# adaLN vectors from w_ada as the moving operand, in column chunks, with q, k, v of the first four attention passes run role by role

## What is computed

```python
ada = silu(c) @ w_ada + b_ada                    # c: 1024 values of this sequence; w_ada: 1024 x 3072
shift, scale, gate = split(ada, 3)
h = rms_norm(x, norm_g) * (1 + scale) + shift
z = h @ w_in                                     # 1024 -> 8704 columns
# branch A: three groups of 8 heads x 64, (window, dilation) = (128,1), (512,4), (2048,16)
q, k = partial_rope(rms_norm(q)), partial_rope(rms_norm(k))
o, lse = dilated_window_attention(q, k, v)       # the groups are combined by their softmax denominators
y_a = attn * silu(z_gateA)
# branch B: chunked spatial gating, y_b = u * (W_s v + b) * silu(z_gateB)
merged = sigmoid(z_mA) * (y_a @ w_branch_a) + sigmoid(z_mB) * (y_b @ w_branch_b)
out = x + gate * (merged @ w_out)
```

## Time and profile before

| what | us |
|---|---|
| median of 6 runs | 961.58 (960.37 to 964.3) |
| the profiled execution, its own time | 961.78 |
| span of its slowest core, first to last instruction | 960.2 |
| PE busy in that span | 812.4 |
| DVE, ACT, POOL busy | 489.4, 409.0, 309.0 |

### The profile page before, as it was taken

How to read it: one execution, slowest core, us unless ns; L and a number is a source line. 1 busy time by engine, 2 the same in 40 slices (tenths; PEclk the granted TensorE clock), 3 DMA queues, 4 the chain that set the end, 5 groups by cost and what they waited for, 6 DMA issues and landing times.

```text
span 960.2 us, 15418 instructions; the slowest of 8 cores (952.5 to 960.2 us)
## 1 busy us (share of the span) xinstructions
PE 812.4 (85%) x5088; PEld 419.4 (44%) x5088; DVE 489.4 (51%) x811; ACT 409.0 (43%) x695; POOL 309.0 (32%) x356
## 2 busy tenths in 40 slices
PE   0895568667899999999999965698876999999997
PEld 0895223233455555544444431243432444444443
DVE  5102346566677777766677654446652432222343
ACT  2103244445466666656666653276663212121100
POOL 0000342344233442332212200624342433332576
PEclk9999887889899999999999987698988999999999
DMA  8980101100082900020000000890005922231396
GB/s 186 335 159 0 44 23 45 45 23 1 1 119 41 151 13 2 1 40 6 2 1 2 1 1 1 91 151 1 1 0 134 218 23 23 23 34 11 117 303 238
DMA packets 53823, 62.63 MB, mean 65 GB/s; under 512 B 31472, under 2 KB 43888, under 8 KB 52720
## 3 DMA queue, kind: packets, MB, share of 16 engines
q0 software_dynamic: 42944, 22.47, 19.3%
q1 hardware_dynamic: 8496, 30.78, 10.4%
q10 hardware_dynamic: 2304, 8.39, 2.1%
HBM read 75.70 MB, written 8.39 MB: 88 GB/s over the span
## 4 chain that ended last, share of the span: by engine, by line
PE 67%; ACT 8%; POOL 7%; DVE 7%; issue 6%; DMA 4%; SPq 1%; DVEq 0%; ACTq 0%; POOLq 0%
PE ps L245 33%; POOL arena L257 6%; PE ps L846 6%; PE ps L848 6%; PE ps L384 6%; DVE arena L257 4%; ACT arena L257 4%; PE ps L850 3%; PE ps L852 3%; PE ps L507 2%; PE ps L545 2%; DMA arena<-w_ada 2%; PE ps L479 2%; PE ps L365 1%; PE ps L549 1%
## 5 line engine op out<-in xcount | busy, mean ns | idle before, releaser
L245 PE MATMUL ps<-arena 128*128 128x512 bf16 x1668 | 419.4, 402 | 27.7 <-DVE arena L257 11.2
L245 PEld LDWEIGHTS ps<-arena 128*128 128x128 bf16 x1668 | 180.3, 116 | 214.3 <-issue 71.9
L257 POOL TENSOR_TENSOR arena<-arena 128x256 f32<-128x256 bf16 (+1 forms) x200 | 109.3, 556 | 356.4 <-DVE arena L257 337.8
L257 ACT ACTIVATE arena<-ps 128x512 bf16<-128x512 f32 (+2 forms) x208 | 138.9, 705 | 179.4 <-PE ps L245 134.0
L257 DVE TENSOR_TENSOR arena<-ps,arena 128x512 bf16<-128x512 f32 (+1 forms) x176 | 123.9, 756 | 37.0 <-ACT arena L257 35.6
L257 DVE TENSOR_REDUCE arena<-arena 128x8 f32<-128x512 bf16 x96 | 65.9, 686 | 73.8 <-ACT arena L257 73.7
L257 ACT ACTIVATE arena<-ps,arena 128x512 bf16<-128x512 bf16 (+1 forms) x112 | 67.9, 652 | 58.3 <-DVE arena L257 41.7
L257 ACT ACTIVATE arena<-arena 128x16 f32<-128x16 f32 (+5 forms) x155 | 65.0, 421 | 63.2 <-DVE arena L257 34.7
L257 DVE TENSOR_TENSOR arena<-arena 128x1024 bf16<-128x1024 bf16 (+4 forms) x138 | 74.1, 544 | 29.2 <-ACT arena L257 26.1
L863 POOL TENSOR_TENSOR arena<-arena 128x512 bf16<-128x512 f32 x32 | 45.6, 1426 | 114.8 <-DVE arena L861 114.8
L384 PE MATMUL ps<-arena 128*128 128x1 f32 x256 | 55.2, 351 | 27.7 <-DMA arena<-w_ada 27.7
(11 more groups left out here) (69 smaller groups left out, 802.2 us busy)
## 6 DMA issues: line engine op xcount, KB each, us to landing
arena<-x SPq DMA_DIRECT2D x32, 512.0 KB, 6.5
arena<-w_in POOLq DMA_DIRECT2D x10, 1024.0 KB, 14.2
arena<-w_ada SPq DMA_DIRECT2D x8, 1024.0 KB, 26.2
out<-arena ACTq DMA_DIRECT2D x16, 512.0 KB, 6.4
arena<-w_in POOLq DMA_DIRECT2D x28, 256.0 KB, 11.5
arena<-w_ada SPq DMA_DIRECT2D x8, 512.0 KB, 8.9
arena<-w_out POOLq DMA_DIRECT2D x2, 1024.0 KB, 27.1
arena<-w_ba POOLq DMA_DIRECT2D x1, 1024.0 KB, 23.5
```

Of the source, the lines that this page charges most:

```text
L245: ins = e.matmul(out_ap, l, r, start=(i == 0), stop=(i == n - 1))
L257: P.op(eng, lambda e: getattr(e, meth)(*a, **kw), reads=reads, writes=writes)
```

## The change

The host lays w_ada's shift and scale columns out as four chunks of 512 columns (256 of shift, 256 of scale), each contiguous for a partition, and w_in as 17 blocks of 512 columns in the same manner; six small inputs become one (`misc`). w_ada's chunks are loaded in nine halves and quarters between the first four tiles of x. `ada_row(c)` turns the matmul round: one column of silu(c) is the stationary operand (128 rows, one column) and 512 columns of w_ada move, in float32, eight matmuls accumulating into one PSUM row; `ada_col` and `ada_tr` split that row into two bfloat16 parts and turn it into columns with one-row matmuls. x is transposed without modulation; the first four tiles stay in PSUM banks 3 to 6 until a chunk's vectors are there and are modulated on the way out, all others are copied out in one operation (`x_evac`) and modulated in place, four tiles at a time (`x_mod4`). The rotary tables' last products move from DVE to POOL.

The first four steps leave the loop: first their q projections with the next four tiles of x between them, then their k projections, then v, with bank names of their own (`zbm`). The loop starts at pass 4; scores and PV belong to step `it-3` instead of `it-2`, so it runs 8 passes past the last step, and `finA` starts at pass 39. In passes 4 to 10 tile `it+5` of x is prepared, and passes 4 to 11 transpose tile `it+4` behind the first scores. The loads of the second group's weights move to the ends of passes 13 to 15.

```diff
-    wada_d = dt("w_ada", [D, 3 * D], F32, kind="ExternalInput").ap()
+    misc_d = dt("misc", [128, 198], F32, kind="ExternalInput").ap()
+    wada_d = dt("w_ada", [128, 4, KC, 512], F32, kind="ExternalInput").ap()
+    wadag_d = dt("w_adag", [D, D], F32, kind="ExternalInput").ap()
...
-    win_d = dt("w_in", [D, IN_COLS], F32, kind="ExternalInput").ap()
-    gqk_d = dt("gqk", [128, 6], F32, kind="ExternalInput").ap()
+    win_d = dt("w_in", [17, 128, KC, 512], F32, kind="ExternalInput").ap()
...
+    def win_v(c0, n):
+        return win_d[c0 // 512][:, :, c0 % 512:c0 % 512 + n]
...
-        dma("sp", cT, cT_d, "cT")
+        dma("sp", misc, misc_d, "misc")
         dma("pool", cst, cst_d, "cst")
         load_w(0, 1536)
+        for c in range(4):
+            for t in range(2):
+                if c < 2:
+                    x_load(2 * c + t)
+            for lo_, hi_ in ([(0, 4), (4, 8)] if c < 3 else [(0, 4), (4, 6), (6, 8)]):
+                dma("sp", wada[:, c, lo_:hi_, :], wada_d[:, c, lo_:hi_, :], "wada%d_%d" % (c, lo_))
+        dma("pool", wslot[1], win_v(2048, 512), "ws1", reads=["wada3_0"])
+        dma("pool", wslot[2], win_v(2560, 512), "ws2", reads=["wada3_6"])
...
+        def x_evac(t, bank):
+            X("dve", "tensor_copy", [B(bank)], ["hT%d" % t], out=hT[:, :, t * 128:(t + 1) * 128], in_=psb[:, bank])
+
+        def x_mod4(n, kc, banked):
+            dst = hT[:, kc, 512 * n:512 * n + 512]
+            if banked:
+                X("dve", "tensor_scalar", [B(3), B(4), B(5), B(6), "ab%d" % (kc // 2)], ["hm%d_%d" % (n, kc)],
+                  out=dst.rearrange("p (t w) -> p t w", t=4), in0=psb[:, 3:7, kc, :], scalar1=ab[:, 8 + kc:9 + kc],
+                  scalar2=ab[:, kc:kc + 1], op0=ALU.mult, op1=ALU.add)
+            else:
+                X("dve", "tensor_scalar", ["hT%d" % t for t in range(4 * n, 4 * n + 4)] + ["ab%d" % (kc // 2)], ["hm%d_%d" % (n, kc)],
+                  out=dst, in0=dst, scalar1=ab[:, 8 + kc:9 + kc], scalar2=ab[:, kc:kc + 1], op0=ALU.mult, op1=ALU.add)
+
+        def ada_row(c):
+            br = c % 2
+            for lo_, hi_ in ([(0, 4), (4, 8)] if c < 3 else [(0, 4), (4, 6), (6, 8)]):
+                def fn(e, lo_=lo_, hi_=hi_):
+                    ins = None
+                    for kc in range(lo_, hi_):
+                        ins = e.matmul(banks[br][0:1, :], sc[:, kc:kc + 1], wada[:, c, kc, :], start=(kc == 0), stop=(kc == 7))
+                    return ins
+                P.op("pe", fn, reads=["wada%d_%d" % (c, lo_), "sc"], writes=[B(br)])
+
...
+            X("act", "copy", [B(br)], ["row%d" % br], out=row[0:1, 0:512], in_=banks[br][0:1, :])
+            X("dve", "tensor_tensor", [B(br), "row%d" % br], ["rowl%d" % br], out=row[0:1, 512:1024], in0=banks[br][0:1, :],
+              in1=row[0:1, 0:512], op=ALU.subtract)
...
+            def fn(e):
+                ins = None
+                for i in range(4):
+                    col = 8 * (i // 2) + 2 * c + i % 2
+                    for hl in range(2):
+                        ins = e.matmul(banks[2][:, col:col + 1], row[0:1, 512 * hl + 128 * i:512 * hl + 128 * i + 128], one11,
+                                       start=(hl == 0), stop=(hl == 1))
+                return ins
+            P.op("pe", fn, reads=["row%d" % br, "rowl%d" % br, "one11", "pT%d" % br], writes=[B(2)])
+            cs = slice(2 * c, 2 * c + 2)
+            abv = ab.rearrange("p (k c) -> p k c", k=2)[:, :, cs]
+            X("dve", "tensor_tensor", [B(2), "gg"], ["ab%d" % c], out=abv, in0=banks[2][:, 0:16].rearrange("p (k c) -> p k c", k=2)[:, :, cs],
+              in1=gg.rearrange("p (k c) -> p k c", k=2)[:, :, cs], op=ALU.mult)
+            X("dve", "tensor_tensor", ["ab%d" % c, "gg"], ["ab%d" % c], out=abv, in0=abv,
+              in1=bb.rearrange("p (k c) -> p k c", k=2)[:, :, cs], op=ALU.add)
+            x_mod4(0, 2 * c, True)
+            x_mod4(0, 2 * c + 1, True)
...
+        def x_in(t, bank):
+            prep_own(t)
+            x_transp(t, bank)
+            x_load(t + 4)
+        ada_row(0)
+        x_in(0, 3)
+        x_in(1, 4)
+        ada_row(1)
+        ada_col(0)
+        x_in(2, 5)
+        x_in(3, 6)
+        ada_tr(0)
+        ada_row(2)
+        ada_col(1)
+        ada_tr(1)
+        prep_own(4)
+        prep_own(5)
+        ada_row(3)
+        ada_col(2)
+        ada_tr(2)
+        ada_col(3)
+        ada_tr(3)
+        for g in (1, 2, 0):
...
+                    X("pool", "tensor_tensor", ["cosT", "misc", "hd"], ["T1_%d" % g], out=T1[:, gi, :, 8 * hf:8 * hf + 8], in0=cg, in1=gv, op=ALU.mult)
+                    X("pool", "tensor_tensor", ["sinT", "misc", "hd"], ["T2_%d" % g], out=T2[:, gi, :, 8 * hf:8 * hf + 8], in0=sg, in1=gv, op=ALU.mult)
...
-        def x_mod(eng, t, bank):
-            v = banks[bank].bitcast(BF16).rearrange("p (j t) -> p j t", j=8)
-            for kc in range(8):
-                dst = hT[:, kc, t * 128:(t + 1) * 128]
-                if eng == "dve":
-                    X("dve", "tensor_scalar", [B(bank), "Acol"], ["hT%d" % t], out=dst, in0=v[:, kc, :], scalar1=Acol[:, kc:kc + 1],
-                      scalar2=Bcol[:, kc:kc + 1], op0=ALU.mult, op1=ALU.add)
...
-        def ada_chunk(kc):
-            def fn(e):
-                ins = None
-                for col in range(16):
-                    ins = e.matmul(banks[2][:, 8 * col + kc:8 * col + kc + 1], wada[:, kc, col * 128:(col + 1) * 128], sc[:, kc:kc + 1],
-                                   start=True, stop=True)
-                return ins
-            P.op("pe", fn, reads=["wada%d" % kc, "sc"], writes=[B(2)])
...
-        for t in range(4):
-            x_square(t, ssx[:, t:t + 1], "ssx%d" % t)
...
-            X("act", "activation", ["rsx%d" % t], ["rsx%d" % t], out=rsx[:, t:t + 1], in_=rsx[:, t:t + 1], func=AF.Exp, scale=-0.5)
-            x_scale("dve", t, rsx[:, t:t + 1], "rsx%d" % t)
-            ada_chunk(t)
-            x_transp(t, 4 + t)
-        for kc in range(4, 8):
-            ada_chunk(kc)
-        X("dve", "tensor_reduce", [B(2)], ["ada"], out=ada[:, 0:16], in_=banks[2][:, 0:128].rearrange("p (c k) -> p c k", k=8),
-          axis=mybir.AxisListType.X, op=ALU.add)
-        X("dve", "tensor_tensor", ["ada", "adab"], ["ada"], out=ada[:, 0:16], in0=ada[:, 0:16], in1=adab[:, 0:16], op=ALU.add)
-        X("dve", "scalar_tensor_tensor", ["ada", "normg"], ["Acol"], out=Acol, in0=ada[:, 8:16], scalar=1.0, in1=normg, op0=ALU.add, op1=ALU.mult)
-        for t in range(4):
-            x_mod(("dve", "act")[t % 2], t, 4 + t)
...
+        zbm = {(1, 0): 6, (2, 0): 7, (3, 0): 2, (1, 1): 4, (2, 1): 5, (3, 1): 0, (0, 2): 1, (1, 2): 6, (3, 2): 0}
...
+        for s in range(4):
+            proj(s, 0)
+            sumsq(s, 0)
+            x_transp(4 + s, TB)
+            x_evac(4 + s, TB)
+            if s < 2:
+                prep_own(6 + s)
+        for kc in range(KC):
+            x_mod4(1, kc, False)
+        x_load(8, gate=["ws2"])
+        for s in range(4):
+            proj(s, 1)
+            sumsq(s, 1)
+            rstd(s)
+            scaleqk(s, 0)
+            scaleqk(s, 1)
+            rope(s)
+        proj(0, 2)
+        vevac(0)
+        transp(0)
+        proj(1, 2)
+        vevac(1)
+        scores(0, 0)
+        mask(0, 0)
+        transp(1)
+        proj(2, 2)
+        vevac(2)
+        scores(0, 1)
+        mask(0, 1)
+        pv(0, 0)
+        accum(0, 0)
+        transp(2)
+        proj(3, 2)
+        vevac(3)
+        pv(0, 1)
+        accum(0, 1)
+        prep_own(8)
+        for t in range(9, 12):
+            x_load(t)
+        x_load(12)
+
         fin_at = {}
         for tb in range(4):
             for hp in range(4):
-                fin_at[32 + 4 * tb + 6 + hp] = (hp, tb)
-        for it in range(NS + 7):
-            a, b_ = it - 1, it - 2
+                fin_at[32 + 4 * tb + 7 + hp] = (hp, tb)
+        for it in range(4, NS + 8):
+            a, b_ = it - 1, it - 3
             A_, T_, S_ = it < NS, 0 <= a < NS, 0 <= b_ < NS
+            xp = it + 5 if it + 5 < NT else None
             if A_:
                 proj(it, 0)
                 sumsq(it, 0)
-                for i, t in enumerate(xtile.get(it - 1, ())):
-                    x_transp(t, TB)
-                    x_mod("dve", t, TB)
-                for i, t in enumerate(xtile.get(it, ())):
-                    x_square(t, ssqk[it % 2][:, 16 + i:17 + i], "ssq%d%d" % (it % 2, 2 + i))
             if S_:
                 scores(b_, 0)
                 mask(b_, 0)
+            if it + 4 < NT:
+                x_transp(it + 4, TB)
+                x_evac(it + 4, TB)
+            if xp:
+                q_ = qi(it)
+                sc_x = x_prep(xp, "pool", ssqk[q_][:, 16:17], rsqk[q_][:, 16:17], "ssq%d2" % q_, "rs%d" % q_, False)
             if A_:
                 proj(it, 1)
                 sumsq(it, 1)
@@ -601,14 +668,17 @@
                 scores(b_, 1)
                 mask(b_, 1)
             if A_:
-                rstd(it)
```

(24 more changed lines are left out.)

301 lines of the change are left out of this document (130 added, 171 removed).

## The result

The changed kernel takes 929.76 us (median of 10 runs, 927.96 to 931.3), the kernel before 962.32 on the same chip (19 runs): ratio 0.9662, 95% interval 0.9651 to 0.9673. Now and then an execution of any of these kernels falls into a slower state of the chip; such runs are left out of all medians and ratios here. The forecast was 908.5: the sign is right and the time lies in the stated range (892 to 937), but it is 21 us off and outside the forecast's own range (895 to 922). The profiled execution's slowest core is core 0, span 925.5 against 960.2: 34.7 gained where 53.3 were forecast.

What follows compares the result with a forecast made beforehand. PE bound the kernel from 262.3 to 559.2 us, but not the setup and early passes before. Pass 12 starting 68.8 earlier, plus 8 for late loads and 7.5 for lag, gave -53.3: 908.5 us, own range 895 to 922, stated 892 to 937.

Steps and rivals of the forecast that it cites:

- first projection: End of the setup: the first projection was to start at 57.8 us (bounds 52 and 64) instead of 95.3.
- steps 0 to 3: The first four steps, as q, k and v rounds, were to take 36.5 us in all instead of 56.4.
- pass 4: First pass of the loop: 10 us (7.9 to 13.8), since its tile of x was prepared ahead.
- passes 5 to 11 with the modulation: Seven passes with a tile of x at 12.6 us, 88.2, plus about 1 for the in-place modulation in pass 11.
- pass 16: Pass in which PE was to wait 6 to 8 us for the second group's later-loaded weights; 8 more (5 to 11).
- third lag: Scores three passes late instead of two: one more drain pass, 7.5 us more (5 to 10).
- behind the barrier: Phases behind the barrier, after the attention: 355.9 us, no change forecast.
- rival (a): Setup: the clock stays at 1.2 GHz through w_ada, first projection 25.4 us later, total 934; chance 0.23.
- (b): Setup: w_ada lands at two thirds of the rate, first projection at 67 us, total 918; chance 0.06.
- (c): Setup: the 64 float32 records don't overlap, 1.52 us each, first projection 67.7 late, total 976; chance 0.05.
- The late loads: Second group's weights loaded two passes later: PE waits for them in pass 16, 8 us more (5 to 11).
- The ring: Passes 5 to 11: PE's transposition and k projection, `rope`, then POOL's scaling in turn; 12.0 us at high clock, 13.3 at low.

## Why the prediction was right, and where it was wrong

By the forecast's own steps, spans of the slowest cores:

| step | forecast | measured | off by |
|---|---|---|---|
| first projection | 57.8 | 62.75 | +4.9 |
| steps 0 to 3 | 36.5 | 34.3 | -2.2 |
| pass 4 | 10 | 8.2 | -1.8 |
| passes 5 to 11 with the modulation | 89.2 | 98.65 | +9.5 |
| passes 12 to 15 | 31.5 | 34.2 | +2.7 |
| pass 16 | 15.9 | 17.5 | +1.6 |
| third lag (passes 17 to 47, and the drain) | +7.5 | +7.6 | +0.1 |
| behind the barrier | 355.9 | 359.9 | +4.0 |

They sum to 18.8; the gain fell short by 18.6 (the rest is rounding). Steps 0 to 3 and pass 4 came 4.0 cheaper than forecast and hide part of the miss. That the time lies in the stated range is luck: the range was drawn up to 937 to take in rival (a), the low clock in the setup, and this rival did not happen.

**Right.** PE is the later one in w_ada, as forecast: from the second half chunk on the records are 0.43 us apart (7.03 for 16, the last of them open for 0.59), the last piece landed at 45.1 (43 forecast) and PE ended at 52.6 (51.6). With that rivals (a), (b) and (c) fall: 0.43 a record was the forecast's pace at 2.4 GHz, w_ada kept its rate, and the records overlap. (Two workings were loose, and neither decides: rival (b)'s 172 GB/s is half of 336, not two thirds, and the v round's four projections of 1.9 and 2 us make 9.6, not 9.) Each tail cost about what it was priced at: with both holds gone the first projection is at 57.71, 57.8 forecast. The late loads and the third lag came about as sized, the loads as two waits, 2.04 for the k weights and 5.01 for the v weights, where one was forecast. Undoing the late loads gave 11.6 back, 8.8 of it by the stage of pass 16. Undoing the third lag gave 3.1 back, as it had also saved 4.3 in steps 0 to 3 and pass 4 that the forecast did not count.

**Wrong, the setup's tail.** "The rotary products on POOL ... done by 57, and `rope` first asks 20 us later": the cover named was for the products' result, and what they do to DVE while they run was put at nothing. They hold it until they are done at 55.55. The forecast also saw that tiles 4 and 5 stand ahead of the third chunk's tail and land behind w_ada, and then let that tail run at 51.6, when PE is done: the wait was named and priced at nothing. Moving one hold left the other (2.3 and nothing that can be told); moving both gave 57.7, the forecast's own time.

**Wrong, passes 5 to 11.** The ring was named rightly, and putting the scaling on DVE proved it. The forecast had 12.0 at the high clock and 13.3 at the low one and took 12.6, the middle, though PE still idles about 3.4 us in a pass. In the run without the in-place modulation the k projection is at the low clock, wholly or in part, in six of the seven passes (2.89 to 3.62), and these take 13.2 to 14.3; in the seventh PE waited least, 2.92, the k projection takes 1.89 and the pass 11.3. The mean is 13.3, so the choice between the two clocks was wrong; the ring's sum at the low clock was right. That is 5 of the 9.5.

**Wrong, the in-place modulation.** In pass 11 it "holds the next q projection by about 1": eight operations of 0.49 are 3.9 us on DVE, at a place where PE needs their result at once; PE waits 4.14 and wakes at 1.2 GHz. Part of the 3.9 is POOL again: the four operations beside `rope` (199.66 to 202.21) are open 0.67 to 0.75, the other four 0.40, and in steps 0 to 3, with POOL idle, the same eight take 2.67 (from 75.11). The pieces that it replaces ran hidden beside the k projection, and do so again when put back; that is worth 6.3, the excess of passes 12 to 15 among it. In pass 7 the same eight operations are nearly free, as PE would otherwise have waited for pass 8's tile.

**Open: behind the barrier.** +4.0 on the slowest core, +3.7 in the mean. PE's wait for the first gating weights is 7.8 on core 0 and 1.5 on core 1 of the same execution; core 2 of the kernel before had 3.9. From the waits of PE after, core 0:

```profile
PE ps L806 <- DMA arena<-w_in: 7.8, 1, 7.8
```

The first of these loads lands 7.1 to 13.9 us after issue, core by core, against 5.8 to 10.1 before, in one execution of each kernel. The layout of w_in does not explain it (352.8 with rows); why they land later was not found, and no run removed it.

## What to carry to other kernels

When work moves to POOL, ask not only who waits for its result but which DVE operations fall into the time in which it runs, above all behind a load on POOL's own queue. In a pass that is a ring across engines, only the links count: 2.85 us of scaling moved from POOL to an engine that does it in 0.75 was worth 29.7, while 2.1 us of modulation on DVE beside the ring, in place of one copy, cost nothing (passes 5 to 11 take 93.4 with it and 93.8 without). A batch that replaces small hidden operations by one large step lands all at once. Where its reader waits for nothing else, the wait is paid twice, in time and in clock.
